# First norm's modulation of a two-block kernel computed in four groups of two operand tiles

## The chip, the cores and the metric

The kernel runs on one core of a Trainium2 chip. The metric is the device time of one execution in microseconds (us), median of the runs; lower is better. Engines: TensorE (PE, with its weight loads as PEld), VectorE (DVE), ScalarE (ACT), GpSimd (POOL) and SyncE (SP), which here issues the transfers.

## What is computed

Only the first norm of the first of two transformer blocks is touched. With D = 1024, S = 512 latent tokens (x) and C = 256 context tokens (ctx):

```python
silu_c = jax.nn.silu(c)
silu_cc = jax.nn.silu(c_ctx)
mod = silu_c @ w_ada[l] + b_ada[l]
mod_c = silu_cc @ w_ada[l] + b_ada[l]
sh1, sc1, gt1, sh2, sc2, gt2 = jnp.split(mod[:, None, :], 6, axis=-1)
h = modulate(rms_norm(x, norm1_g[l]), sh1, sc1)
hc = modulate(rms_norm(xc, norm1_g[l]), csh1, csc1)
... = split_in_proj(h @ w_in[l])
```

`modulate` multiplies by 1 plus the scale and adds the shift. The first norm needs the shift and the scale of layer 0: 2048 columns of `w_ada`, for the two vectors silu(c) and silu(c_ctx). Everything behind the input projection stays as it is.

## The kernel before

**Layout.** Features lie on the 128 partitions, so x is `xL`, eight operand tiles (k = 0 to 7, KD = 8) of 128x512, and ctx is `xC`, eight of 128x256; T = 768 columns together. A full-precision product is made of three products of rounded parts: an operand is split in `high` (rounded) and `low` (the rest), a weight unit in `w_high` and `w_low`. A weight unit is 128x1024 (512 KB), the weights of one output tile for all eight k. It comes through a ring of four (RING = 4) and is split into one of two places (SPLIT = 2): ScalarE copies it to `w_high` (L456), VectorE subtracts to `w_low` (L459).

**First block of code** (L832 to L890). SP issues `small`, `const`, `cond` (the conditioning vectors), x, ctx, then the 16 units of `w_ada` (512 KB each, L646), then four weight units. ScalarE applies silu to `cond`, squares x and ctx (L885), and VectorE adds the squares (L868). TensorE forms the mean (L851), ScalarE an approximate inverse root (L888), VectorE refines it in three steps (L828 to L830) and multiplies every x tile by it into `hL`, `hC` (L874). In between TensorE sums the products of `cond` with `w_ada` (class `Modulation`, L662), 16 matmuls per four units, all into one bank of PSUM. When all 16 units are summed, ScalarE copies the rows out (L676), TensorE turns them into columns (L670: rows to columns by a product with a constant), VectorE adds the bias (L690) and makes the gain from the scale (L696). "Turn" below is this second product.

**The barrier.** Each `nc.Block()` is closed by a barrier of all five engines: nobody, SP included, starts the next block's code until all have reached the end of this one.

**The input projection** (class `Stage`, `input_projection`). Its `normed` part is `Shifted` (L1006): for every k ScalarE makes `high` from `hL`, the gain and the shift. For k in `by_scalar` (2, 4, 6) ScalarE modulates in place (L1025), then rounds (L1028), and VectorE only subtracts (L1043); for the others ScalarE makes `high` in one step (L1031) while VectorE modulates in place (L1040) and subtracts. TensorE (L494, `gemm_tensor`) makes the products of the output tiles 0 and 1 as operands come, tile 1 two operand tiles behind tile 0:

```python
for j in range(n + 2):
    if j < n:
        product(*one, j)
    if j >= 2:
        product(*two, j - 2)
```

One `product` is six matmuls: three pairs of parts, each for 512 and 256 columns. The other 26 tiles follow one by one.

Of the kernel before, what the change touches and what calls it, by code (L numbers as in the profile page):

```python
# [313 lines left out]
def build(nc, dram, where, where1, where2, where3, n_units):  # L314
    with ExitStack() as ctx:
# [156 lines left out]
        def gemm_tensor(pe, g, inner=(), late=None):  # L472
# [31 lines left out]
            if g.paired and g.first == 0:  # L504
# [114 lines left out]
        ada_landed = [count(f"ada_landed{n}") for n in range(5)]  # L619
        ada_used, rows_out, groups_in, mod_out = (count(n) for n in ("ada_used", "rows_out", "groups_in", "mod_out"))  # L620

        class Modulation:

            gpsimd = sync = None
            BANK_AT = 7 * BANK

            def __init__(self, l, block0, blocks, when, places=()):
                self.l, self.block0, self.blocks, self.when, self.places = l, block0, blocks, when, places
                self.units = 2 * blocks
                assert len(when) == self.units and blocks <= 16
                self.last = when[-1]
                self.hooks = self.last + 4

            def load(self, sync, n):
                slot = n % len(self.places)
                if n >= len(self.places):  # L640
                    sync.wait_ge(ada_used.sem, ada_used.at(n - len(self.places) + 1))
                src = dram["ada"][(self.l * 6 * D // ADA_COLS + self.block0) * 2 + n]
                dst = self.places[slot]
                if len(dst.shape) == 3:
                    src = src.rearrange("p (k c) -> p k c", c=ADA_COLS)
                sync.dma_start(dst, src).then_inc(self.landed(n).sem, 16)  # L646

            def landed(self, n):
                return ada_landed[n // 4]

            def wait_landed(self, engine, n):

                engine.wait_ge(self.landed(n).sem, self.landed(n).at(16 * 4))

            def tensor_parts(self, pe, t):
                for n in range(self.units):
                    if self.when[n] == t:
                        self.wait_landed(pe, n)
# [19 lines left out]
            def vector_parts(self, dve, t):  # L678
                if t == self.last + 3:
                    dve.wait_ge(groups_in.sem, groups_in.at(1))  # L680
                    self.finish_columns(dve, ps[:, self.BANK_AT + ADA_COLS:self.BANK_AT + ADA_COLS + 64], 1)

# [2445 lines left out]
```

## Time and profile before

| | |
|---|---|
| runs: median (lowest to highest) | 3451.77 us (3448.72 to 3457.12), n = 3 |
| the profiled execution: its own time | 3454.18 us |
| its span, first to last instruction | 3452.2 us |
| mean granted TensorE clock | 0.989 of full speed |
| TensorE busy | 3307.5 us (96%) |
| VectorE, ScalarE, GpSimd busy | 1771.3 (51%), 1203.1 (35%), 445.2 (13%) us |
| product 0 of the input projection starts | 45.04 us |
| output tile 2 starts | 64.07 us |

Times in the trace count from the first instruction. In a timeline a line is a start, a duration, the engine, the source line, what it writes and reads, how many such instructions were merged, and in brackets the idle time before it with what ended it. In a table of stretches the busy time of each engine is followed by its instruction count, and PEclk is the granted TensorE clock as a share of 2.4 GHz (1.00 is 2.4, 0.50 is 1.2 GHz).

### The profile page before, as it was taken

Reading aid. Unit: us, or ns where it says so; the run is one execution under the profiler, and the core shown is the slowest. Engines: PE = TensorE matmul, PEld = TensorE weight load, DVE = VectorE, ACT = ScalarE, POOL = GpSimd, SP = SyncE. Lnnn points to the kernel's source line nnn. Section 1 sums busy time; section 2 is a strip of 40 time slices with the busy share of each in tenths; the row PEclk is TensorE's granted clock in tenths of the full one; section 3 lists DMA queues with packets and bytes.
Section 4 is the critical chain, followed back from the end, with each engine's and each line's share of the span. In section 5 each row is a group of like instructions: output and inputs, shape, how many; then the busy total and the mean of one; then the engine's idle time right before and its main releaser. Section 6 shows DMA issues by size and latency. Waiting matters only on the chain. (4 is left out here: it accounts for less than half of the span.)

```text
span 3452.2 us, 49601 instructions
## 1 busy us (share of the span) xinstructions
PE 3307.5 (96%) x20432; PEld 2652.1 (77%) x20432; DVE 1771.3 (51%) x2736; ACT 1203.1 (35%) x2054; POOL 445.2 (13%) x477
## 2 busy tenths in 40 slices
PE   6999999999999999999999999999999998899998
PEld 4887778788888787776887867667888777578886
DVE  5874657654132456655323357654443385744433
ACT  3214762321131222753223333353332332532322
POOL 0211111000000021114500133120000022200000
PEclk9999999999999999999999999999999999999999
DMA  6420013354122122012222321012223220022232
GB/s 243 147 99 18 2 50 141 129 188 141 62 68 68 55 86 68 2 50 89 97 92 94 102 84 58 26 43 92 96 94 104 98 86 3 31 98 92 96 100 80
DMA packets 78265, 290.66 MB, mean 84 GB/s; under 512 B 8672, under 2 KB 9056, under 8 KB 77280
## 3 DMA queue, kind: packets, MB, share of 16 engines
q1 hardware_dynamic: 78048, 287.55, 24.5%
q8 instruction: 163, 2.67, 0.3%
q14 instruction: 54, 0.44, 0.0%
HBM read 285.42 MB, written 2.10 MB: 83 GB/s over the span
## 5 line engine op out<-in xcount | busy, mean ns | idle before, releaser
L459 DVE TENSOR_TENSOR w_low<-ring,w_high 128x1024 fp32r<-128x1024 f32 x418 | 526.7, 1260 | 1351.8 <-ACT w_high L456 1351.2
L494 PE MATMUL ps<-arena_r,w_high 128*128 128x512 f32 x3568 | 1142.1, 385 | 11.1 <-PEq L1517 9.2
L456 ACT ACTIVATE w_high<-ring 128x1024 fp32r<-128x1024 f32 x418 | 442.9, 1060 | 1517.9 <-PE ps L494 1508.8
L494 PEld LDWEIGHTS ps<-arena_r,w_high 128*128 128x128 f32 x3568 | 646.1, 188 | 163.7 <-issue 16.7
L494 PE MATMUL ps<-low,w_high 128*128 128x512 f32 (+1 forms) x2448 | 764.7, 361 | 0.0
L494 PE MATMUL ps<-high,w_high 128*128 128x512 f32 x2368 | 737.0, 362 | 15.0 <-DVE low L992 7.0
L494 PE MATMUL ps<-high,w_low 128*128 128x512 f32 x2368 | 730.7, 359 | 0.0
L494 PE MATMUL ps<-arena_r,w_low 128*128 128x512 f32 (+1 forms) x1456 | 545.6, 387 | 0.0
L494 PEld LDWEIGHTS ps<-low,w_high 128*128 128x128 f32 x2448 | 411.7, 189 | 74.8 <-issue 1.1
L494 PEld LDWEIGHTS ps<-high,w_high 128*128 128x128 f32 x2368 | 395.2, 188 | 95.8 <-issue 12.0
L494 PEld LDWEIGHTS ps<-high,w_low 128*128 128x128 f32 x2368 | 395.0, 188 | 70.3
L494 PEld LDWEIGHTS ps<-arena_r,w_low 128*128 128x128 f32 x1456 | 266.6, 189 | 61.3
L555 POOL TENSOR_TENSOR tmp<-tmp 128x512 f32<-128x512 f32 (+1 forms) x42 | 67.3, 1604 | 1527.5 <-ACT tmp L545 1527.5
L1634 ACT ACTIVATE probs<-ps,stat 128x512 f32<-128x512 f32 (+3 forms) x224 | 152.5, 690 | 74.7 <-DVE stat L1592 38.8
L1535 PE MATMUL ps<-arena 64*128 64x256 f32 (+6 forms) x784 | 143.3, 439 | 24.3 <-ACT probs L1634 17.2
L1551 PE MATMUL ps<-const,probs 128*128 128x128 f32 x896 | 125.5, 283 | 13.6 <-ACT probs L1625 6.5
L1551 PEld LDWEIGHTS ps<-const,probs 128*128 128x128 f32 x896 | 100.4, 144 | 49.1 <-DVE probs L1607 36.9
L802 DVE CUSTOM_DVE_ANT_0 arena<-arena 128x1024 f32<-128x1024 f32 x104 | 137.1, 1363 | 0.0
L1535 PEld LDWEIGHTS ps<-arena 64*128 64x128 f32 (+1 forms) x784 | 82.4, 193 | 67.4 <-issue 32.8
L1625 ACT ACTIVATE probs<-ps 128x512 f32<-128x512 f32 (+3 forms) x224 | 121.2, 598 | 22.2 <-PE ps L1551 21.4
L494 PE MATMUL ps<-low,w_low 128*128 128x512 f32 x368 | 127.5, 374 | 0.0
L1564 PE MATMUL ps<-probs,arena 128*64 128x128 f32 x1792 | 123.1, 280 | 2.8 <-ACT hL L1646 2.2
(353 smaller groups left out, 2905.8 us busy)
## 6 DMA issues: line engine op xcount, KB each, us to landing
ring<-in_weights SPq DMA_DIRECT2D x428, 512.0 KB, 3.3
arena<-in_ada_rows SPq DMA_DIRECT2D x80, 512.0 KB, 3.9
arena<-in_ada SPq DMA_DIRECT2D x16, 512.0 KB, 15.5
arena<-in_cond_rows SPq DMA_DIRECT2D x3, 1024.0 KB, 5.8
xL<-in_x SPq DMA_DIRECT2D x1, 2048.0 KB, 10.9
out<-xL SPq DMA_DIRECT2D x4, 512.0 KB, 2.7
low_f<-in_low_rank SPq DMA_DIRECT2D x3, 512.0 KB, 4.2
const<-in_const SPq DMA_DIRECT2D x1, 1104.0 KB, 5.4
```

Of the source, the lines that this page charges most:

```text
L456: act.activation(w_high[:, slot, :], ring[:, place, :], ACT.Copy).then_inc(unit_high.sem, 1)
L459: dve.tensor_tensor(w_low[:, slot, :], ring[:, place, :], w_high[:, slot, :].bitcast(F32), ALU.subtract).then_inc(unit_free.sem, 1)
L494: mm = pe.matmul(bank(4 * (t % 2) + 2 * p + s, width), w, g.split[k][s][x], start=(n == 0 and m == 0), stop=(n == len(part) - 1 and m == 2))
L555: pool.tensor_tensor(tmp[:, 1, 0:total], tmp[:, 1, 0:total], tmp[:, 0, 0:total], ALU.add).then_inc(squares_sum.sem, 1)
L802: ins = dve.tensor_tensor_reduce(out, self.slots[place], self.vectors[s], 1.0, 0.0, ALU.mult, ALU.add, mod[:, to, s:s + 1])
L1535: mm = pe.matmul(ps[:, to:to + w], q, k, start=True, stop=True)
L1551: mm = pe.transpose(ps[:, to:to + P], probs[:, j % 3, e, m * P:m * P + P], con("ident"))
L1564: mm = pe.matmul(ps[e * HD:e * HD + HD, O_AT:O_AT + P], pair["values"][e][m], probs[:, j % 3, e, m * P:m * P + P], start=(m == 0 and not b ...
L1625: act.activation(probs[:, j % 3, e, 0:keys], ps[:, turned_at(j, e):turned_at(j, e) + keys], ACT.Copy).then_inc(turned_out.sem, 1)
L1634: act.activation(probs[:, i % 3, e, 0:keys], ps[:, scores_at(i, e):scores_at(i, e) + keys], ACT.Exp, bias=st[:, 2 + e:3 + e], scale=-1.0, ...
```

## The change

The class `FirstModulation` and the class `Shifted` go; a class `Opening` takes the place of both. The 2048 columns are eight blocks of 256, blocks 0 to 3 the shift and 4 to 7 the scale. Group g (0 to 3) takes block g and block 4 + g, four units of `w_ada`, which give shift and scale of the operand tiles 2g and 2g + 1.

- First block of code: x and ctx are issued first, then `small`, `const`, `cond`, the four units of group 0 and one weight unit. ScalarE squares first and applies silu afterwards. The sums of the modulation and the multiplications by the inverse root are no longer in this block.
- Input projection: SP issues the units of group 1, a weight unit, the units of groups 2 and 3, two weight units. TensorE sums and turns groups 0 and 1, then makes the products; the sums and the turn of group 2 stand ahead of k = 2, those of group 3 ahead of k = 4. Tiles 0 and 1 now go side by side for each k.
- GpSimd multiplies the odd tiles by the inverse root, VectorE the even ones, each ahead of its group's columns. `by_scalar` is (2, 4, 5, 6).

```diff
+            if g.opening:
+                for t in range(2):
+                    begin(t)
+                for k in range(KD):
+                    g.opening.before(pe, k)
+                    for t in range(2):
+                        product(t, 0, k)
+                for t in range(2):
+                    beside(t)
+                done = 2
+            elif g.paired and g.first == 0:
...
+        class Opening:
...
+            by_scalar = (2, 4, 5, 6)
...
+            def open(self, pe, g):
+
+                pe.wait_ge(ada_landed[g].sem, 16 * 4)
+                for m in range(2):
+                    for half in range(2):
+                        unit = self.places[4 * g + 2 * m + half]
+                        for j in range(4):
+                            mm = pe.matmul(ps[32 * j:32 * j + 32, self.region(g):self.region(g) + ADA_COLS],
...
+                mm.then_inc(ada_summed.sem, 1)
+                pe.wait_ge(rows_out.sem, g + 1)
+                for h in range(2):
+                    at = self.region(g) + ADA_COLS + 32 * h
+                    mm = pe.matmul(ps[:, at:at + 32], rows[:, h * P:h * P + P], con("groups"), start=True, stop=True)
+                mm.then_inc(groups_in.sem, 1)
+
+            def tensor(self, pe):
+                for g in range(1 + self.ahead):
+                    self.open(pe, g)
+
+            def before(self, pe, k):
+                g = k // 2 + self.ahead
+                if k % 2 == 0 and k and g < OPEN:
+                    self.open(pe, g)
...
+            def scalar(self, act, gemms, first):
+                for g in range(self.ahead):
+                    self.take_rows(act, g)
+                for g in range(OPEN):
+                    if g + self.ahead < OPEN:
+                        self.take_rows(act, g + self.ahead)
+                    if g == 0:
+                        split_unit(act, None, 0, 0, None, 0)
+                    act.wait_ge(opened.sem, g + 1)
+                    for k in (2 * g, 2 * g + 1):
+                        self.high(act, k, gemms[0].split[k])
+                        if k == 0:
+                            split_unit(act, None, 1, 1, None, 0)
...
+            def vector(self, dve, gemms, first):
+                for g in range(OPEN):
+                    for at, w, x, h in ((0, S, xL, hL), (S, C, xC, hC)):
+                        dve.tensor_tensor(h[:, 2 * g, :], x[:, 2 * g, :], tmp[:, 0, at:at + w], ALU.mult)
+                    self.columns(dve, g)
...
+            def sync(self, sync):
+                for g in range(1, OPEN):
+                    opening.load(sync, g)
+                    load_units(sync, min(g + 1, 2))
+                load_units(sync, RING)
...
+        opening = Opening()
+        opening.ahead = 1
...
             def _(sync):
+                sync.dma_start(xL[:, :, :], dram["x"]).then_inc(tokens_in.sem, 16)
+                sync.dma_start(xC[:, :, :], dram["ctx"]).then_inc(tokens_in.sem, 16)
                 sync.dma_start(small[:, :], dram["small"]).then_inc(params_in.sem, 16)
                 sync.dma_start(const[:, :], dram["const1"]).then_inc(params_in.sem, 16)
                 sync.dma_start(cond[:, :, :], dram["cond"]).then_inc(params_in.sem, 16)
-                sync.dma_start(xL[:, :, :], dram["x"]).then_inc(tokens_in.sem, 16)
-                sync.dma_start(xC[:, :, :], dram["ctx"]).then_inc(tokens_in.sem, 16)
-                first_mod.sync(sync)
-                load_units(sync, RING)
+                opening.load(sync, 0)
+                load_units(sync, 1)
                 sync.wait_ge(params_in.sem, 48)
```

**SP, at the end of the first block.** Before, all of `w_ada` (L646) and the four weight units stand ahead of the barrier:

```order
L646 DMA arena<-in_ada 128x1024 x16
L431 DMA ring<-in_weights 128x1024 x4
L832 UNCONDITIONAL_BRANCH [waits params_in]
L1290 UNCONDITIONAL_BRANCH [waits barrier_Pool_Activation_PE_DVE_SP_release]
L431 DMA ring<-in_weights 128x1024 [waits unit_free]
```

Now (L764 loads `w_ada`, L431 weight units):

```order
L764 DMA arena<-in_ada 128x1024 x4
L431 DMA ring<-in_weights 128x1024
L901 UNCONDITIONAL_BRANCH [waits params_in]
L1300 UNCONDITIONAL_BRANCH [waits barrier_Pool_Activation_PE_DVE_SP_release]
L764 DMA arena<-in_ada 128x1024 x4
L431 DMA ring<-in_weights 128x1024
L764 DMA arena<-in_ada 128x1024 x8
L431 DMA ring<-in_weights 128x1024 x2
```

Groups 1 to 3, 12 of the 16 units, moved behind the barrier.

**ScalarE, from the start of the input projection, now.** L797 copies a group's rows out, L810 makes `high` in one step, L804 and L807 modulate and round:

```order
L1312 UNCONDITIONAL_BRANCH [waits barrier_Pool_Activation_PE_DVE_SP_release]
L797 ACTIVATE rows<-ps 128x256 [waits ada_summed] x2
L456 ACTIVATE w_high<-ring 128x1024 [waits unit_landed0]
L810 ACTIVATE high<-hL,mod,gain 128x512 [waits opened]
L810 ACTIVATE high<-hC,mod,gain 128x256
L456 ACTIVATE w_high<-ring 128x1024 [waits unit_landed1]
L810 ACTIVATE high<-hL,mod,gain 128x512 [waits odd_made]
L810 ACTIVATE high<-hC,mod,gain 128x256
L797 ACTIVATE rows<-ps 128x256 [waits ada_summed]
L804 ACTIVATE hL<-hL,mod,gain 128x512 [waits opened]
L804 ACTIVATE hC<-hC,mod,gain 128x256
L807 ACTIVATE high<-hL 128x512 [waits chain_s]
```

The copies of groups 0 and 1 stand ahead of the first weight unit's split and of k = 0; the copy of group 2 ahead of k = 2, that of group 3 (further on, in the same way) ahead of k = 4.

**TensorE, around the second operand tile's end, now.** L776 sums, L783 turns, L494 is a product; the first row is the last matmul of k = 1 for tile 1:

```order
L494 MATMUL ps<-high,w_low 128x256
L776 MATMUL ps<-arena,cond 32x256 [waits ada_landed2]
L776 MATMUL ps<-arena,cond 32x256 x15
L783 MATMUL ps<-const,rows 128x32 [waits rows_out]
L783 MATMUL ps<-const,rows 128x32
L494 MATMUL ps<-high,w_high 128x512 [waits low_ready]
```

Group 2's sums stand in TensorE's queue behind all four products of k = 0 and 1. Before, no product of the projection had a sum between it and the next.

## Rows read from the trace of the kernel before

**Rows 1.** Page, busy time by engine, and a stretch behind the opening
```profile
PE 3307.5 (96%) x20432; PEld 2652.1 (77%) x20432; DVE 1771.3 (51%) x2736; ACT 1203.1 (35%) x2054; POOL 445.2 (13%) x477
...
50.00:60.00 10.00, 10.00 (x59) 8.86 (x58) 6.67 (x14) 5.15 (x10) 0.00 (x0) 1.00 0.20 80
```
**Rows 2.** TensorE's timeline, sums of the modulation (L662) and the turn (L670)
```profile
20.80 3.64 PE L662 MATMUL ps<-arena,cond 128*32 128x256 f32 x32 [20.80 <-DMA arena<-in_ada]
...
30.94 1.93 PE L662 MATMUL ps<-arena,cond 128*32 128x256 f32 x32 [0.54 <-DMA arena<-in_ada]
...
36.05 3.44 PE L662 MATMUL ps<-arena,cond 128*32 128x256 f32 x32 [3.18 <-DMA arena<-in_ada]
...
40.01 0.63 PE L670 MATMUL ps<-const,rows 128*128 128x32 f32 x4 [0.51 <-ACT rows L676]
```
**Rows 3.** Timeline, from the last sum to the first two products
```profile
39.57 0.38 ACT L676 ACTIVATE rows<-ps 128x256 f32<-128x256 f32 x1 [10.47 <-PE ps L662]
...
41.10 0.24 DVE L696 SCALAR_TENSOR_TENSOR gain<-mod,small 128x8 f32<-128x8 f32 x2
41.62 0.81 ACT L1031 ACTIVATE high<-hL,mod,gain 128x512 fp32r<-128x512 f32 x1 [0.72 <-PEq L832]
...
45.04 0.98 PE L494 MATMUL ps<-high,w_high 128*128 128x512 f32 x2 [4.40 <-DVE low L1043]
...
47.09 1.00 PE L494 MATMUL ps<-high,w_high 128*128 128x512 f32 x2
```
**Rows 4.** Stretches of two us around the sums and first products; columns end PEclk, DMA share, GB/s
```profile
36.00:38.00 2.00, 1.95 (x20) 0.99 (x24) 2.00 (x5) 0.00 (x0) 0.00 (x0) 0.50 1.03 412
...
46.00:48.00 2.00, 2.00 (x8) 1.50 (x7) 1.99 (x3) 1.97 (x5) 0.00 (x0) 0.50 1.00 414
...
50.00:52.00 2.00, 2.00 (x13) 1.79 (x12) 2.00 (x5) 2.00 (x5) 0.00 (x0) 1.00 0.93 381
```
**Rows 5.** Transfers: KB each, median us from issue to landing
```profile
cond<-in_cond SPq DMA_DIRECT2D x1, 248.0 KB, 6.5
...
ring<-in_weights SPq DMA_DIRECT2D x428, 512.0 KB, 3.3
```
**Rows 6.** Timeline of the first block: ScalarE's squares, VectorE's sums, the root's last step
```profile
15.56 0.63 ACT L885 ACTIVATE hL<-xL 128x512 f32<-128x512 f32 x1 [6.78 <-DMA xC<-in_ctx]
...
17.36 0.69 DVE L868 TENSOR_TENSOR tmp<-hL 128x512 f32<-128x512 f32 x1 [9.02 <-ACT hC L885]
...
24.76 0.42 DVE L868 TENSOR_TENSOR tmp<-tmp,hC 128x256 f32<-128x256 f32 x1
...
31.12 0.96 DVE L830 SCALAR_TENSOR_TENSOR tmp<-tmp 128x768 f32<-128x768 f32 x1
```
**Rows 7.** SP's waits, 0 to 50 us: for whom, total, times, longest
```profile
SPq L832 <- PEq L832: 15.7, 1, 15.7
```
**Rows 8.** Groups by form: VectorE's modulation to 66 us, GpSimd's nearest rows in the span
```profile
L1040 DVE TENSOR_SCALAR hL<-hL,gain,mod 128x512 f32<-128x512 f32 x5 | 2.7, 545 | 0.5 <-ACT high L1031 0.4
...
L1040 DVE TENSOR_SCALAR hC<-hC,gain,mod 128x256 f32<-128x256 f32 x5 | 2.0, 410 | 0.0
...
L555 POOL TENSOR_TENSOR tmp<-tmp 128x512 f32<-128x512 f32 (+1 forms) x42 | 67.3, 1604 | 1527.5 <-ACT tmp L545 1527.5
```
**Rows 9.** Timeline, making of the operand tile k = 4 by ScalarE and VectorE
```profile
48.34 0.80 ACT L1025 ACTIVATE hL<-hL,mod,gain 128x512 f32<-128x512 f32 x1
...
50.20 0.40 ACT L1028 ACTIVATE high<-hC 128x256 fp32r<-128x256 f32 x1
...
51.47 0.42 DVE L1043 TENSOR_TENSOR low<-hC,high 128x256 fp32r<-128x256 f32 x1
```
**Rows 10.** Timeline, third weight unit and output tile 2
```profile
61.09 1.06 ACT L456 ACTIVATE w_high<-ring 128x1024 fp32r<-128x1024 f32 x1 [5.91 <-PE ps L494]
62.18 1.23 DVE L459 TENSOR_TENSOR w_low<-ring,w_high 128x1024 fp32r<-128x1024 f32 x1 [5.04 <-ACT w_high L456]
...
64.07 0.61 PE L494 MATMUL ps<-high,w_high 128*128 128x512 f32 x2
```

More of the change, by code:

```diff
@@ L503, in gemm_tensor @@
             done = 0
-            if g.paired and g.first == 0:
+            if g.opening:
[9 more added lines that the diff above has]
+            elif g.paired and g.first == 0:
                 one, two = ((0, 0), (0, 1)) if len(g.parts) == 2 else ((0, 0), (1, 0))
@@ L706, in build @@
-        class FirstModulation(Modulation):
-            def sync(self, sync):
-                for n in range(self.units):
-                    self.load(sync, n)
+        OPEN = 4
+        ada_landed = [count(f"ada_landed{n}") for n in range(OPEN)]
+        ada_summed, rows_out, groups_in, bias_in, opened, odd_made = (
+            count(n) for n in ("ada_summed", "rows_out", "groups_in", "bias_in", "opened", "odd_made"))
         cond_in, cond_made, row_used = (count(n) for n in ("cond_in", "cond_made", "row_used"))
@@ L871, in _ @@
                 inverse_root(dve, tmp[:, 0, :], ps[:, 5 * BANK:5 * BANK + T], EPS, tmp[:, 1, :])
-                for k in range(KD):
-                    for at, w, x, h in ((0, S, xL, hL), (S, C, xC, hC)):
-                        dve.tensor_tensor(h[:, k, :], x[:, k, :], tmp[:, 0, at:at + w], ALU.mult)
-                for t in range(first_mod.hooks):
-                    first_mod.vector_parts(dve, t)
             @block.scalar
             def _(act):
-                act.wait_ge(params_in.sem, 48)
-                act.activation(cond[:, :, :], cond[:, :, :], ACT.Silu).then_inc(left_s.sem, 1)
                 act.wait_ge(tokens_in.sem, 32)
@@ L886, in _ @@
                     ins.then_inc(squares_in.sem, 1)
+                act.wait_ge(params_in.sem, 48)
+                act.activation(cond[:, :, :], cond[:, :, :], ACT.Silu).then_inc(left_s.sem, 1)
                 act.wait_ge(pe_ready.sem, 1)
@@ L1169, in __init__ @@
                     g.made, g.own = made, 0 if made else len(g.split)
+                    g.opening = None
                 first = 0
@@ L1349, in input_projection @@
                 gemms.append(g)
-            return Stage(gemms, ToZ(), normed, inner=[Heads(l), *also])
+            stage = Stage(gemms, ToZ(), normed, beside, inner=[Heads(l), *also])
+            if normed is opening:
+                gemms[0].opening = opening
+            return stage
         values_turned, values_out, sq_out, mean_in, mean_read, root_out, normed_out = (count(n) for n in (
@@ L1996, in build @@
                      [(19, 0, 2 * KD, 3 * KD, 2 * KD, 2, 1)], True, 18)
-        project([input_projection(0, Shifted(lambda k, s: gain[:, 0, k, s:s + 1], lambda k, s: mod[:, k, s:s + 1]), [CondRows(cond0, 0), rows0])])
+        project([input_projection(0, opening, [CondRows(cond0, 0), rows0], FirstLoads())])
         for l in range(DEPTH):
```

198 lines of the change are left out of this document (76 added, 122 removed).

## The prediction

> **What bounds the kernel.** I read the page first, then the table of stretches, the waits and the timeline up to 66 us. TensorE is busy for 96% of the span, and from the first products on it has no idle time: a stretch of ten us behind the opening has 10.00 us of it [rows 1]. So the kernel is an opening, in which TensorE waits, and then a queue of products. What the opening costs is the time at which output tile 2 starts. All behind it hangs on TensorE's tiles (weights, evictions, later sums), so a shift of that start goes one to one into the end.
>
> The opening before is bound by transfers. The sums of 16 matmuls wait for `w_ada` three times; the last begin at 36.05 and end at 39.49 [rows 2]. Rows and turn follow, the gain is ready at 41.34, ScalarE's first `high` starts at 41.62, and the first product stands at 45.04 [rows 3].
>
> **What moves, in order of time.** All times are those of the trace of before, from the first instruction.
>
> *Tokens first.* `small`, `const` and `cond` are 126 + 1104 + 248 KB, 1.51 MB; at 0.41 MB per us (last column of [rows 4]) x and ctx land 3.7 us sooner, at 11.8 instead of 15.5. But VectorE waits for `cond` ahead of its sums, and that was there at 8.15 (1.65 + 6.5 [rows 5]) and now lands last of the five, at 15.5. Its sums start at 15.7 instead of 17.36 [rows 6]: a gain of 1.7 us, not 3.7. They end at 23.5, the root's last step 6.9 us later as before (25.18 to 32.08 [rows 6]), at 30.4. Silu and its table load on ScalarE lie in these sums and cost nothing; without that cover they would cost about 2 us.
>
> *The barrier.* SP now issues group 0 and one weight unit and waits. That it does wait is seen before: 15.7 us at the block's end, at no cost, since all transfers were issued [rows 7]. Now groups 1 to 3 are issued only when the root is done, at 30.4 + 0.3 (41.34 to 41.62 is such a passage [rows 3]) = 30.7. The queue has run dry meanwhile. A 512 KB transfer takes 3.3 us to land [rows 5], each further one 1.28 us at 410 GB/s: group 1 lands at 30.7 + 3.3 + 3 x 1.28 = 37.9.
>
> *First product.* Group 0 is summed meanwhile. Group 1's sums stand ahead of the products on TensorE, and its copy ahead of the first split and `high` on ScalarE. Its sums take 1.93 us at 2.4 and 3.44 at 1.2 GHz [rows 2, 4]; TensorE has idled before, so I take 3.44: 41.4. The copy takes 0.46 (39.49 to 39.95 [rows 2, 3]), the split 1.06, and from ScalarE's first `high` to the product are 3.42 [rows 3]: 46.4 instead of 45.04, **1.4 us later**.
>
> *GpSimd's multiplications.* Their cost is bounded by 0 and by 8 x 1.6 = 13 us [rows 8]: from 30.7 they end at 44 at the latest, the one for k = 1 at 34, when ScalarE wants it at 45. Nothing; without this cover, up to 3 us.
>
> *In the groups.* A product takes 2.05 us at 1.2 GHz (45.04 to 47.09 [rows 3]) and half, 1.03, at 2.4. k = 0 and 1 are four products, the first two at the low clock: 46.4 to 52.6. Behind them TensorE sums group 2, 1.93 us, to 54.5. Only then can ScalarE copy the rows (0.46), and behind the copy in its queue stands the making of k = 2, although its gain may be long there: 48.34 to 50.60 in the row, 2.3 us, then VectorE's subtraction and the hand-over, 1.2 [rows 9]. TensorE has nothing in this time but the turn (0.6): a gap of 3.95 us, new. k = 2 and 3 take 4.1, with operands in time: for k = 3 ScalarE needs 1.3 and VectorE 0.96 + 1.1 [rows 6, 8], which is a product pair's 2.06. The same comes again ahead of k = 4. Ahead of k = 6 no sums are left, but VectorE multiplies and makes the columns only behind the `low` of k = 5 (1.0 + 0.7 [rows 2, 3, 6]), and then the 2.3 and 1.2 run again: 5.2 us less the 2.06 of products, a gap of 3.15. Last, the third weight unit's split waits for tile 0. It takes 2.3 us (61.09 to 63.41 [rows 10]; tile 2 then started at 64.07); before, three products of tile 1 covered it, now one does: 1.3 us.
>
> **Sum.** Later start 1.4; sums inside the products 2 x 1.93 = 3.9; gaps 2 x 3.95 + 3.15 = 11.05; third unit 1.3; together 17.6. To this comes the clock. Before, idle times of 3.18 and 4.40 us were both followed by 0.50 in PEclk [rows 2, 3, 4], and the products from 45.04 ran at 1.2 GHz for their first four us, a loss of 2 us. The gaps here are as long, two of them broken by the turn. Bounds: none falls, 0; all three fall, 6. I take two of three at 1.6, 3.2, since the gaps are nearest to the one of 3.18, after which the 3.44 of the sums cost 1.5 over 1.93. The sum is **+20.8 us**.
>
> On the clock the Trainium skill ("TensorE: Matmul & The Clock Gate", section "HAM oscillation — how this bites in real kernels") speaks against this change: a loop that computes briefly and then waits falls back to the low clock at each wait. The trace agrees as far as it goes (both its idle times). By the rule all three gaps fall, and the sum would be 23.6 instead of 20.8.
>
> The profiled execution has 3454.18 us, so 3475.0; it stands 2.4 above the median of the runs, to which the change is compared: **3472**.
>
> **Rivals.** A measurement of this kernel can tell 0.3%, 10.4 us, from no change.
>
> *A, the forecast:* chance 0.65. Its own bounds: no fall of the clock (-3.2), group 1 summed at 2.4 GHz (-1.5), transfers 1 us quicker or slower, three falls (+2.8), 2 us from GpSimd and the first copies: 3464 to 3480.
>
> *B, the low clock stays all through the opening.* The 14 products that I put at 1.03 take 2.05, +14, and the two sums inside +3, less the 3.2: 3486. For it: a rise took four us of unbroken work at 45 us, and no stretch here is longer. Against it: the products from 45.04 on were at 1.00 in the stretch from 50 us [rows 4], and those from 46.4 on follow each other here without a pause just as long. 0.10.
>
> *C, group 1 isn't waited for*, because SP passes the barrier or its transfers start at once (then the change's barrier does not do what the order says). Then the first product would come when group 0's sums (34.2) are copied, turned and used: 34.2 + 2.1 + 3.4 = 39.7, 6.7 sooner; 3465. Against it is SP's wait [rows 7]. Still slower, since gaps and sums stay. 0.12.
>
> *D, no change: the gaps close.* The place is ScalarE's queue ahead of k = 2, 4 and 6. If the rows come out and the operand tiles are made while TensorE still has products or sums, the 11 us of gaps and the 3.2 of clock go: 3458, within 0.3%; with C as well 3451. It decides at 2 us: the copy, `high` and `low` would have to end within the sums they wait for. For it: ScalarE is only half busy [rows 1]. Against: the copy waits for the sums' end, and 0.46 + 2.3 + 1.2 follow one upon the other. 0.09.
>
> *E, transfers bind.* Groups 2 and 3 land at 44 and 49, 8 and 13 us ahead of their sums, w2 and w3 at 50 and 52. They would have to run at under half of 410 GB/s: 3480 or more. 0.04.
>
> **Numbers.** Range 3461 to 3483: A with its bounds, C, and the upper edge of E; outside are B and D. Faster by over 0.3% (under 3441) no case gives: 0.01. Within 0.3%: D and a little of C, 0.10. Slower: 0.89.
>
> **What would show it.** Right: SP's first `w_ada` transfer behind the barrier at 31 us; first product at 46 to 47; ahead of k = 2 and k = 4 an idle time of TensorE of 3 to 4 us in two pieces around the turn, ended by the copy and by `low`; one of about 3 ahead of k = 6; tile 2 starting at 82 to 86; from there equal spacing of tiles. Wrong: a first product under 42 (C); gaps under 1 us (D); PEclk 0.50 over all of 46 to 80 (B); sums of groups 2 and 3 that wait for transfers (E); or tile 2 at its old place relative to the end, with the difference made elsewhere.

## The result, and the profile after

| | before | after |
|---|---|---|
| runs: median (lowest to highest) | 3449.55 us (3447.78 to 3457.12), n = 5 | 3471.82 us (3465.57 to 3472.75), n = 5 |
| profiled execution: own time, span | 3454.18, 3452.2 us | 3472.75, 3471.0 us |
| mean granted TensorE clock | 0.989 | 0.990 |
| product 0 of the input projection | 45.04 us | 45.88 us |
| output tile 2 starts | 64.07 us | 83.47 us |
| ScalarE's table load inside the projection (L1424, now L1437) | 126.64 us | 147.58 us |

The ratio is 1.0055, with a 95% interval of 1.004 to 1.007: slower by 14 to 24 us. The last row of the table is used as a mark below: it is one instruction of the projection, the same in all kernels here, and what stands ahead of it is the opening and the first tiles.

The page of the changed kernel has TensorE's busy time almost unchanged (3307.5 before [rows 1]); the first slices carry the difference:

```profile
span 3471.0 us, 49648 instructions
...
PE 3310.5 (95%) x20444; PEld 2659.2 (77%) x20444; DVE 1767.9 (51%) x2744; ACT 1206.5 (35%) x2060; POOL 453.8 (13%) x485
```

TensorE's timeline of the changed kernel, 18 to 95 us, answers to [rows 2, 3, 10]; L776 are sums, L783 turns, L494 products:

```profile
22.82 2.90 PE L918 MATMUL ps<-tmp,const 128*128 128x512 f32 x4 [22.82 <-DVE tmp L934]
30.17 3.64 PE L776 MATMUL ps<-arena,cond 128*32 128x256 f32 x32 [4.45 <-PEq L901]
34.30 1.06 PE L783 MATMUL ps<-const,rows 128*128 128x32 f32 x4 [0.49 <-ACT rows L797]
37.54 3.64 PE L776 MATMUL ps<-arena,cond 128*32 128x256 f32 x32 [2.18 <-DMA arena<-in_ada]
41.69 1.06 PE L783 MATMUL ps<-const,rows 128*128 128x32 f32 x4 [0.50 <-ACT rows L797]
45.88 0.98 PE L494 MATMUL ps<-high,w_high 128*128 128x512 f32 x2 [3.13 <-DVE low L860]
...
51.78 1.93 PE L776 MATMUL ps<-arena,cond 128*32 128x256 f32 x32
54.22 0.63 PE L783 MATMUL ps<-const,rows 128*128 128x32 f32 x4 [0.50 <-ACT rows L797]
57.43 1.01 PE L494 MATMUL ps<-high,w_high 128*128 128x512 f32 x2 [2.58 <-DVE low L860]
...
64.31 1.93 PE L776 MATMUL ps<-arena,cond 128*32 128x256 f32 x32
66.75 0.63 PE L783 MATMUL ps<-const,rows 128*128 128x32 f32 x4 [0.50 <-ACT rows L797]
69.97 1.01 PE L494 MATMUL ps<-high,w_high 128*128 128x512 f32 x2 [2.58 <-DVE low L860]
...
76.98 0.61 PE L494 MATMUL ps<-high,w_high 128*128 128x512 f32 x2 [1.11 <-DVE low L860]
...
83.47 1.01 PE L494 MATMUL ps<-high,w_high 128*128 128x512 f32 x2 [2.04 <-DVE arena L1344]
```

Read it from the brackets. The sums of group 1 end a wait for a transfer, at 37.54. Ahead of k = 2 (57.43) and k = 4 (69.97) the same pattern stands twice: sums, 0.50 us of waiting for ScalarE's copy, the turn, 2.58 us of waiting for a `low` tile. Ahead of k = 6 it is 1.11 us, and tile 2 waits 2.04 us for VectorE's eviction of tile 0 (L1344). None of these waits was there before, between 45.04 and 64.07.

ScalarE's timeline of the changed kernel shows the order that makes the gap: the copy comes first, then the tile whose gain has long been there.

```profile
45.33 0.59 ACT L810 ACTIVATE high<-hC,mod,gain 128x256 fp32r<-128x256 f32 x1
53.78 0.38 ACT L797 ACTIVATE rows<-ps 128x256 f32<-128x256 f32 x1 [7.87 <-PE ps L776]
54.06 0.80 ACT L804 ACTIVATE hL<-hL,mod,gain 128x512 f32<-128x512 f32 x1
...
55.92 0.40 ACT L807 ACTIVATE high<-hC 128x256 fp32r<-128x256 f32 x1
```

It was idle for 7.87 us, the last 3.6 of them with the gain of group 1 ready: VectorE had it at 50.19.

```profile
49.96 0.23 DVE L841 SCALAR_TENSOR_TENSOR gain<-mod,small 128x2 f32<-128x2 f32 x2
```

The table of stretches shows the clock behind three of the gaps:

```profile
58.00:60.00 2.00, 2.00 (x8) 1.68 (x7) 1.97 (x5) 0.00 (x0) 0.00 (x0) 0.50 0.21 84
70.00:72.00 2.00, 2.00 (x6) 1.71 (x7) 0.95 (x3) 0.99 (x3) 0.00 (x0) 0.50 0.00 0
84.00:86.00 2.00, 2.00 (x8) 1.65 (x7) 0.00 (x0) 2.00 (x3) 0.00 (x0) 0.50 0.69 242
```

The column misses one stretch at the low clock. The row of the first products reads 1.00:

```profile
46.00:48.00 2.00, 2.00 (x7) 1.72 (x8) 1.97 (x4) 0.00 (x0) 0.00 (x0) 1.00 1.03 412
```

But from 46.66 to 49.22 one pair of matmuls follows the other every 0.64 us, as it does where the column has 0.50, and from 49.61 on every 0.35 us, as it does where the column has 1.00. So these products, too, began at 1.2 GHz.

**The sum of it up to the mark** (147.58 - 126.64 = 20.9 us). I split the time from the first product to the mark in stretches of 1 us and added up TensorE's idle time, and its busy time times the share of the clock that was missing (busy at PEclk 0.50 counts half as loss): idle 9.3 us against 0.0 before, clock 5.9 against 2.2, the rest 86.4 against 79.4. With the first product 0.8 us later that is 0.8 + 9.3 + 3.8 + 7.0 = 20.9. Of the 7.0, the two sums and turns inside the products are 2 x (1.93 + 0.63) = 5.1, and 1.5 are clock as well, from the stretch that the column misses: the first six pairs of matmuls took 3.73 us (45.88 to 49.61), six pairs at 2.4 GHz took 2.19 (76.98 to 79.17). So the clock's loss up to the mark is 7.5 us, 5.3 more than before; 0.4 us are left over.

Behind the mark the two profiled executions differ in something that the change doesn't touch. Between the marks at 289.47 and 482.93 us before, and 310.40 and 500.25 after, the distance falls from 20.9 to 17.3 us. The stretch there is the start of the attention, before:

```profile
295.00:305.00 10.00, 8.85 (x45) 7.04 (x43) 5.05 (x11) 5.20 (x13) 0.00 (x0) 0.50 0.00 0
```

and after:

```profile
316.00:326.00 10.00, 7.97 (x58) 6.34 (x57) 6.23 (x14) 6.47 (x15) 0.29 (x1) 0.83 0.00 0
```

The kernel before stayed at 1.2 GHz for these ten us, the changed one for a part of them. In the nine experiments below the ten us at the same place, of the same code, have 0.53 to 0.89. From the mark to the end the eleven profiled executions take 3318.9 to 3325.6 us, and the one of the kernel before is the longest. So the experiments are read by tile 2 and the mark, where effects of 2 us show, and only then by the time.

### The profile page after: what moved, and what is told of

Its sections match the earlier page's. It is cut to its first block and busy times, and to the rows that moved or that the text cites. A ratio compares the mean times of both kernels' runs of the same rounds, so it can differ in the third digit from the quotient of the medians.

```text
span 3471.0 us, 49648 instructions
## 1 busy us (share of the span) xinstructions
PE 3310.5 (95%) x20444; PEld 2659.2 (77%) x20444; DVE 1767.9 (51%) x2744; ACT 1206.5 (35%) x2060; POOL 453.8 (13%) x485
## 5 line engine op out<-in xcount | busy, mean ns | idle before, releaser
L494 PE MATMUL ps<-arena_r,w_high 128*128 128x512 f32 x3568 | 1143.3, 386 | 11.1 <-PEq L1530 9.1
L494 PEld LDWEIGHTS ps<-arena_r,w_high 128*128 128x128 f32 x3568 | 647.2, 188 | 162.5 <-issue 16.7
L494 PE MATMUL ps<-low,w_high 128*128 128x512 f32 (+1 forms) x2448 | 767.4, 362 | 0.0
L494 PE MATMUL ps<-high,w_high 128*128 128x512 f32 x2368 | 739.7, 363 | 23.5 <-DVE low L860 9.4
L494 PE MATMUL ps<-high,w_low 128*128 128x512 f32 x2368 | 732.5, 360 | 0.0
L494 PE MATMUL ps<-arena_r,w_low 128*128 128x512 f32 (+1 forms) x1456 | 546.4, 388 | 0.0
L494 PEld LDWEIGHTS ps<-high,w_high 128*128 128x128 f32 x2368 | 397.1, 189 | 103.0 <-issue 10.9
L494 PEld LDWEIGHTS ps<-low,w_high 128*128 128x128 f32 x2448 | 413.8, 190 | 74.5 <-issue 1.1
L494 PEld LDWEIGHTS ps<-high,w_low 128*128 128x128 f32 x2368 | 396.8, 189 | 70.2
L494 PEld LDWEIGHTS ps<-arena_r,w_low 128*128 128x128 f32 x1456 | 267.1, 189 | 61.1
L494 PE MATMUL ps<-low,w_low 128*128 128x512 f32 x368 | 127.6, 375 | 0.0
```

Of the source, the lines that this page charges most:

```text
L494: mm = pe.matmul(bank(4 * (t % 2) + 2 * p + s, width), w, g.split[k][s][x], start=(n == 0 and m == 0), stop=(n == len(part) - 1 and m == 2))
```

## The experiments

All times of the mark, tile 2 and first product are from the profiled executions. The ratios compare medians. For the changed kernel the kernel before had 3449.55 us (n = 5); in the experiments it was measured again beside each of them and had 3452.1 to 3452.6 (n = 12 to 21). Against these the changed kernel's median is 19 to 20 us over, not 22.

| kernel | first product | tile 2 | mark | span | ratio to before, interval |
|---|---|---|---|---|---|
| before | 45.04 | 64.07 | 126.64 | 3452.2 | |
| changed | 45.88 | 83.47 | 147.58 | 3471.0 | 1.0055, 1.004 to 1.007 |
| transfers ahead | 43.60 | 80.98 | 143.55 | 3463.8 | 1.0036, 1.0021 to 1.005 |
| and all groups first | 49.66 | 77.83 | 140.40 | 3460.6 | 1.0031, 1.002 to 1.0043 |
| tile 1 lags | 46.81 | 85.05 | 147.62 | 3469.3 | 1.004, 1.0026 to 1.0055 |
| gaps filled | 46.41 | 83.92 | 146.49 | 3466.9 | 1.0054, 1.0038 to 1.0071 |
| before, tokens first | 46.05 | 65.80 | 128.37 | 3450.0 | 1.0001, 0.9992 to 1.0011 |
| spread | 39.06 | 66.82 | 129.39 | 3454.0 | 1.0004, 0.9995 to 1.0013 |
| spread, no GpSimd | 35.77 | 60.41 | 123.00 | 3441.9 | 0.9984, 0.9975 to 0.9993 |
| changed, sums don't wait | 45.45 | 82.63 | 145.22 | 3468.6 | 1.0039, 1.0024 to 1.0054 |
| spread, both | 35.07 | 58.17 | 120.75 | 3443.5 | 0.9978, 0.9968 to 0.9987 |

### 1. The transfers ahead of the barrier

```diff
                 opening.load(sync, 0)
                 load_units(sync, 1)
+                for g in range(1, OPEN):
+                    opening.load(sync, g)
+                    load_units(sync, min(g + 1, 2))
+                load_units(sync, RING)
                 sync.wait_ge(params_in.sem, 48)
```

> The changed kernel with the transfers of groups 1 to 3 and of the weight units issued in the first block, ahead of the barrier. Theory (late start from group 1's transfers is one of three costs, gaps and sums inside the products the others): group 1 is there when group 0 is turned, its sums start at about 35.4 us instead of 37.5, run partly at 2.4 GHz, first product at 42.5 to 44 instead of 45.9, gaps of TensorE ahead of k = 2 and 4 as before (about 3.7 us), tile 2 at 80 to 82 instead of 83.5: 2 to 3 us less than the changed kernel, about 17 us over the kernel before. Rival (the barrier makes most of the loss): first product near 40, gaps gone or short because the later groups are early, at most 8 us over the kernel before.

TensorE's timeline of this kernel, groups 1 and 2:

```profile
35.35 3.55 PE L776 MATMUL ps<-arena,cond 128*32 128x256 f32 x32
39.41 0.63 PE L783 MATMUL ps<-const,rows 128*128 128x32 f32 x4 [0.51 <-ACT rows L797]
43.60 0.98 PE L494 MATMUL ps<-high,w_high 128*128 128x512 f32 x2 [3.56 <-DVE low L860]
...
56.03 1.01 PE L494 MATMUL ps<-high,w_high 128*128 128x512 f32 x2 [2.58 <-DVE low L860]
```

Group 1's sums wait for no transfer any more (35.35 instead of 37.54), the first product comes 2.3 us sooner, tile 2 2.5 us, the mark 4.0 us. The wait of 2.58 us ahead of k = 2 is the same to the last digit. So the late transfers cost 2.3 to 2.5 us. The other 1.5 us at the mark are the clock, which this time didn't fall behind the wait ahead of tile 2: from tile 2 to the mark it is 62.57 us instead of 64.11. The rival that gives the barrier most of the loss falls: 16.9 us are left at the mark, and the median is 12.4 over that of the kernel before, where the rival had at most 8.

### 2. All four groups ahead of the products

```diff
             def region(self, g):
-                return (7, 3)[g % 2] * BANK
+                return (7, 3, 6, 2)[g] * BANK
...
-        opening.ahead = 1
+        opening.ahead = 3
```

on top of experiment 1.

> As the kernel with the early transfers, and in addition the sums and turns of all four groups stand ahead of the first product (four regions of PSUM instead of two). Theory (the chain sums, copy, operand, low part between the products is the main cost): first product later, at 48 to 50 us, but no sums and no gap over 0.5 us ahead of k = 2, 4, 6; tile 2 at 70 to 72; 6 to 9 us over the kernel before, so some 12 us less than the changed kernel although its products start later. Rival (the later start and transfers are the cost, the gaps come from slow operand making on ScalarE and VectorE): gaps of 3 us stay ahead of each even k, 20 us or more over the kernel before.

TensorE's timeline of this kernel:

```profile
49.66 0.98 PE L494 MATMUL ps<-high,w_high 128*128 128x512 f32 x2 [3.56 <-DVE low L860]
57.39 0.61 PE L494 MATMUL ps<-high,w_high 128*128 128x512 f32 x2 [2.02 <-DVE low L860]
64.34 0.62 PE L494 MATMUL ps<-high,w_high 128*128 128x512 f32 x2 [2.49 <-DVE low L860]
71.34 0.62 PE L494 MATMUL ps<-high,w_high 128*128 128x512 f32 x2 [2.50 <-DVE low L860]
```

A first product 6.1 us later than in experiment 1, and yet tile 2 3.2 us sooner. From the first product to tile 2 it is 28.2 us instead of 37.4: sums, copies and turns between the products cost 9.2 us, the falls of the clock behind their waits included. But I expected no gap, and 2.0 to 2.5 us are left ahead of every even k. ScalarE's timeline of this kernel names who is late:

```profile
54.00 0.82 ACT L804 ACTIVATE hL<-hL,mod,gain 128x512 f32<-128x512 f32 x1 [4.31 <-DVE gain L841]
...
60.95 0.81 ACT L804 ACTIVATE hL<-hL,mod,gain 128x512 f32<-128x512 f32 x1 [3.47 <-DVE gain L841]
```

It waits for the gain, though all columns were turned by 46.1 us: VectorE multiplies tile k and makes the columns only behind the `low` of the tile ahead. So there are two chains: sums, copy, operand (TensorE to ScalarE), and low, multiplication, columns, operand (VectorE to ScalarE). Taking the first away brings the time from k = 1's end to k = 2's start from 5.65 us in the changed kernel (51.78 to 57.43) down to 2.0. The median is 10.9 us over the kernel before, where I expected 6 to 9.

### 3. Tile 1 two operand tiles behind

```diff
-                for k in range(KD):
+                for k in range(KD + 2):
                     g.opening.before(pe, k)
-                    for t in range(2):
-                        product(t, 0, k)
+                    if k < KD:
+                        product(0, 0, k)
+                    if k >= 2:
+                        product(1, 0, k - 2)
```

> The changed kernel with tile 1 two operand tiles behind tile 0, as in the kernel before, nothing else. Theory (the third unit's split and tile 0's eviction are covered by one product of tile 1 where three covered them): the idle 2.0 us ahead of tile 2 go, and the fall of the clock behind it; the gaps ahead of k = 2 and 4 shrink a little or stay, since fewer products stand behind the sums; tile 2 at 80 to 81.5 at 2.4 GHz, 3 to 4 us less than the changed kernel over the opening. Rival (the idle time is the silu or the transfer of the unit): tile 2 still starts 2 us behind the last product of tile 1.

A miss: tile 2 starts at 85.05, where I expected 80 to 81.5. The idle 2.04 us ahead of tile 2 did go, with the low clock behind them, as expected. But the mark stands where it did (147.62; 0.9 us of it is group 1, which landed later in this execution: its sums began at 38.48 instead of 37.54). With the lag, only two products stand ahead of group 2's sums, the others behind the gap, and the gap stays at 2.58 us:

```profile
49.70 1.01 PE L494 MATMUL ps<-high,w_high 128*128 128x512 f32 x2 [0.63 <-DVE low L862]
...
51.91 3.18 PE L778 MATMUL ps<-arena,cond 128*32 128x256 f32 x32
55.61 0.63 PE L785 MATMUL ps<-const,rows 128*128 128x32 f32 x4 [0.51 <-ACT rows L799]
58.82 1.01 PE L494 MATMUL ps<-high,w_high 128*128 128x512 f32 x2 [2.58 <-DVE low L862]
```

The sums took 3.18 instead of 1.93 us, since the clock had not risen by then. Up to the mark TensorE is idle for 7.8 us instead of 9.3, and the clock's loss is 8.1 instead of 7.5. So 0.6 of the 1.5 us that the lag saved went to the clock and the other 0.9 to the late group 1.

### 4. The gaps filled with matmuls

```diff
                 if k % 2 == 0 and k and g < OPEN:
                     self.open(pe, g)
+                    for m in range(3):
+                        pe.matmul(bank(6), con("mean_all"), const[:, 0:BANK], start=True, stop=True)
```

> The changed kernel with three matmuls of 512 columns into an unused bank behind the turns of groups 2 and 3, so that TensorE works through the two long gaps (2.6 us of 2.4 GHz work each). Theory (the clock falls in the gaps and costs 2 to 3 us in each): PEclk stays 1.00 from 50 to 75 us, the products of k = 2 to 5 take 1.03 us each, tile 2 at 79 to 80 instead of 83.5, 3 to 5 us less. Rival (the clock's fall is hidden since operands are the bound at either clock): tile 2 where it is, 83.5, or later by what the added matmuls delay.

TensorE's timeline of this kernel; L795 are the added matmuls:

```profile
55.72 0.63 PE L783 MATMUL ps<-const,rows 128*128 128x32 f32 x4 [0.50 <-ACT rows L799]
56.18 2.82 PE L795 MATMUL ps<-const 128*128 128x512 f32 x6
58.93 0.61 PE L494 MATMUL ps<-high,w_high 128*128 128x512 f32 x2
...
63.31 1.93 PE L776 MATMUL ps<-arena,cond 128*32 128x256 f32 x32
...
68.96 0.61 PE L494 MATMUL ps<-high,w_high 128*128 128x512 f32 x2
...
75.97 1.01 PE L494 MATMUL ps<-high,w_high 128*128 128x512 f32 x2 [2.49 <-DVE low L862]
```

The clock held 1.00 from 54 to 74 us, as meant. From group 2's sums to group 3's it is 10.0 us (53.28 to 63.31) instead of 12.5 (51.78 to 64.31): the first fall's price, 2.5 us. From group 3's sums to k = 6 it is 12.7 us with and without the fill (63.31 to 75.97, 64.31 to 76.98): the products are quicker, and the gap ahead of k = 6 is longer, 2.49 instead of 1.11. There the rival holds, operands are the bound. Tile 2 is 0.45 us later, the mark 1.1 sooner; this execution's first product was 0.5 later and its first four products ran 1 us longer at the low clock. But the clock now fell behind the longer gap:

```profile
76.00:78.00 2.00, 2.00 (x6) 1.71 (x7) 1.88 (x4) 0.05 (x1) 0.00 (x0) 0.50 0.00 0
```

From k = 6 to tile 2 it is 7.95 us instead of 6.49, and with that 1.5 us more; from tile 2 to the mark, where the clock stayed up, it is 62.57 instead of 64.11, 1.5 us less. So a fall costs 1.5 to 2.5 us where TensorE is the bound behind it, and nothing where a later wait shrinks by as much; filling the two gaps moved one fall to k = 6.

### 5. The kernel before with the tokens first

The kernel before, x and ctx ahead of `small`, `const` and `cond`, squares ahead of silu:

```diff
+                sync.dma_start(xL[:, :, :], dram["x"]).then_inc(tokens_in.sem, 16)
+                sync.dma_start(xC[:, :, :], dram["ctx"]).then_inc(tokens_in.sem, 16)
                 sync.dma_start(small[:, :], dram["small"]).then_inc(params_in.sem, 16)
...
-                sync.dma_start(xL[:, :, :], dram["x"]).then_inc(tokens_in.sem, 16)
-                sync.dma_start(xC[:, :, :], dram["ctx"]).then_inc(tokens_in.sem, 16)
```

> The kernel before with one part of the change alone: x and ctx issued first, squares ahead of silu. Theory (the opening of the kernel before is bound by the last group's landing, which no order of the same bytes moves): the root is done 2 us sooner, the last sums still start at 36.0 and the first product at 45.0; no change, within 3 us. Rival (the tokens are the bound): first product and end 2 us or more sooner.

The root's last step starts at 28.70 instead of 31.12, and nothing comes of it: the last sums start at 36.44 after a wait of 3.57 us for `w_ada`, the first product at 46.05. 1.0001, interval 0.9992 to 1.0011. The part of the change that is a gain by itself is worth nothing while the last unit's landing is the bound.

### 6. The groups with their order spread

All transfers ahead of the barrier, group 0 summed and turned in the first block, sums and turns apart, copies behind a tile that is made, GpSimd multiplying tiles 1 to 7, tile 1 two behind:

```diff
             def tensor(self, pe):
-                for g in range(1 + self.ahead):
-                    self.open(pe, g)
+                self.sums(pe, 1)
+                self.sums(pe, 2)
+                self.turn(pe, 1)

             def before(self, pe, k):
-                g = k // 2 + self.ahead
-                if k % 2 == 0 and k and g < OPEN:
-                    self.open(pe, g)
+                if k == 1:
+                    self.turn(pe, 2)
+                if k == 2:
+                    self.sums(pe, 3)
+                if k == 4:
+                    self.turn(pe, 3)
...
+                for k in range(KD):
+                    if k % 2 == 0:
+                        act.wait_ge(opened.sem, k // 2 + 1)
+                    self.high(act, k, gemms[0].split[k])
+                    if k == 0:
+                        self.take_rows(act, 1)
+                        split_unit(act, None, 1, 1, None, 0)
+                    if k == 1:
+                        self.take_rows(act, 2)
+                    if k == 3:
+                        self.take_rows(act, 3)
```

> The changed kernel with its groups kept and the order rewritten: all transfers ahead of the barrier, group 0 summed and turned in the first block, sums and turn of a group at separate places (sums of 1 and 2 and turn of 1 ahead of k = 0, turn of 2 ahead of k = 1, sums of 3 ahead of k = 2, turn of 3 ahead of k = 4), ScalarE's copies behind a tile that is already made, GpSimd multiplying tiles 1 to 7, tile 1 two behind. Theory (the groups can gain once nothing on ScalarE waits for sums that stand behind products): first product at 35 to 37 us, no gap over 1 us except at the start, tile 2 at 57 to 60 instead of 64.07, 4 to 7 us under the kernel before (0.1 to 0.2%). Rival 1 (ScalarE and VectorE can't make operands in the products' time with GpSimd's part beside them): gaps of 1 to 2 us per tile, tile 2 at 64 or later, no gain. Rival 2 (sums through the transfers bind): sums of group 2 or 3 wait, tile 2 at 62.

17 us sooner at tile 2 than the changed kernel, and no different from the kernel before (1.0004, 0.9995 to 1.0013). The first rival shows, in a form that I hadn't thought of. VectorE's timeline of this kernel, the `low` tile of k = 0 beside GpSimd and that of k = 2 after it:

```profile
34.14 1.50 DVE L862 TENSOR_SCALAR hL<-hL,gain,mod 128x512 f32<-128x512 f32 x1
...
36.42 1.63 DVE L865 TENSOR_TENSOR low<-hL,high 128x512 fp32r<-128x512 f32 x1
...
38.84 2.30 DVE L459 TENSOR_TENSOR w_low<-ring,w_high 128x1024 fp32r<-128x1024 f32 x1
...
48.81 0.69 DVE L865 TENSOR_TENSOR low<-hL,high 128x512 fp32r<-128x512 f32 x1 [2.34 <-ACT high L817]
```

The same instructions take 0.54, 0.69 and 1.22 us when GpSimd stands still. GpSimd worked from 31.18 to 48.3, and TensorE waited 5.15 us for the `low` tile of k = 1 at 45.85 (the text recorded for experiment 7 calls it the third operand tile; it is the second).

### 7. The same without GpSimd

```diff
+            def turned(self, dve, k):
+                for at, w, x, h in ((0, S, xL, hL), (S, C, xC, hC)):
+                    ins = dve.tensor_tensor(h[:, k, :], x[:, k, :], tmp[:, 0, at:at + w], ALU.mult)
+                ins.then_inc(odd_made.sem, 1)
...
             def gpsimd(self, pool):
-                for k in range(1, KD):
-                    for at, w, x, h in ((0, S, xL, hL), (S, C, xC, hC)):
-                        ins = pool.tensor_tensor(h[:, k, :], x[:, k, :], tmp[:, 0, at:at + w], ALU.mult)
-                    ins.then_inc(odd_made.sem, 1)
+                pass
```

> The spread kernel with all multiplications by the inverse root on VectorE, none on GpSimd. Theory (GpSimd's eight-odd multiplications slowed VectorE's instructions beside them, 0.69 to 1.63 us for a 128x512 subtraction, and that made the 5 us gap ahead of its third operand tile): VectorE's subtractions stay at 0.69 us from 31 to 48 us, first product at 36 instead of 39, last low part at 56 to 57 instead of 62.4, tile 2 at 59 to 61 instead of 66.8; 3 to 5 us under the kernel before. Rival (VectorE was the bound by its own work, and seven more multiplications of 0.94 us make it worse): tile 2 at 67 or later, no gain.

VectorE's timeline of this kernel, the instructions of the fence above:

```profile
33.70 0.54 DVE L868 TENSOR_SCALAR hL<-hL,gain,mod 128x512 f32<-128x512 f32 x1
...
34.60 0.69 DVE L871 TENSOR_TENSOR low<-hL,high 128x512 fp32r<-128x512 f32 x1
...
35.54 1.22 DVE L459 TENSOR_TENSOR w_low<-ring,w_high 128x1024 fp32r<-128x1024 f32 x1
```

With seven more multiplications on VectorE its last `low` tile is done at 55.98 instead of 62.37, tile 2 starts at 60.41, and the kernel is faster than the one before: 0.9984, interval 0.9975 to 0.9993. At the mark it is 3.6 us ahead. Beside the multiplications one thing more differs: VectorE makes the columns of group 2 one tile sooner. That GpSimd slowed VectorE is shown by the single instructions; how much of the 6.4 us at tile 2 is the columns is not shown.

### 8. The changed kernel, sums not waiting for the parameters

```diff
-                dve.wait_ge(params_in.sem, 48)
-
-                dve.tensor_tensor(col("attn0", 0, KD), col("final1", 0, KD), col("attn0", 0, KD), ALU.mult)
...
+                dve.wait_ge(params_in.sem, 48)
+
+                dve.tensor_tensor(col("attn0", 0, KD), col("final1", 0, KD), col("attn0", 0, KD), ALU.mult)
                 dve.wait_ge(act_ready.sem, 1)
```

> The changed kernel with VectorE's wait for the parameters, and the small product behind it, moved behind the sums of squares. Theory (of the 3.7 us by which the tokens land sooner, this wait takes two): sums from 12.8 us, at their end by 20.7, mean at 20.8, barrier, first w_ada transfer behind it and first product 2 us sooner (28.0 and 43.8), tile 2 at 81 to 82; 2 us less than the changed kernel. Rival (silu and the two table loads on ScalarE or the constants for the mean are next and give only part): 1 us or less.

Between the two expectations. The sums started only 1.1 us sooner, at 13.73 instead of 14.86, since the tokens landed 0.8 us later in this execution (squares from 11.94, not 11.09), and the root gained those 1.1 us. Group 1 was issued 1.1 us sooner (29.00) and landed no sooner (sums at 37.46), so the first product gained 0.4. The mark is 2.4 us sooner, of which 1.5 are the clock, which didn't fall ahead of tile 2 (62.59 us from there to the mark, not 64.11). The step isn't settled by this kernel; in the next one, where the tokens landed in time, the mean comes 2.0 us sooner.

### 9. Both

Experiment 7 with the edit of experiment 8.

> The kernel without GpSimd's multiplications with the parameters' wait moved as well. Theory: root and first product another 2 us sooner (34), last operand tiles bound by VectorE's own queue from there, tile 2 at 57.5 to 59; 5 to 7 us under the kernel before, 0.15 to 0.2%. Rival (group 2's and 3's landing at 31 and 36 us is next): the sums of group 2 wait on transfers and tile 2 stands where it does without this edit.

The mean starts at 20.87 instead of 22.90. The first product gains only 0.7 us of that: its `low` tile is there at 33.59, but group 2's sums, which wait 0.36 us for their transfer (the rival, small), and the turn of group 1 stand ahead of it to 35.1. Tile 2 starts at 58.17, 2.2 us sooner than in experiment 7; 1.5 of these are the clock, which fell there behind a wait of 2.17 us ahead of k = 1 and here doesn't. The mark is at 120.75, 5.9 us ahead of the kernel before. In the table of stretches of this kernel the clock stays up from 35 to 55 us, and TensorE is busy for 17.6 of these 20 us:

```profile
35.00:45.00 10.00, 8.19 (x69) 6.17 (x69) 9.69 (x32) 6.43 (x13) 0.00 (x0) 1.00 1.02 410
45.00:55.00 10.00, 9.43 (x55) 7.86 (x54) 7.03 (x20) 5.49 (x10) 0.00 (x0) 1.00 0.21 84
```

Median 3443.72 us against 3452.1, ratio 0.9978, interval 0.9968 to 0.9987. It has the lowest median of all kernels here, though its interval and that of experiment 7 overlap. VectorE is what is full now (9.69 of 10 us up to 45). Of the 8.4 us, 5.9 stand at the mark; the rest is behind it and not explained by the edits.

## Why the prediction was right

The forecast was 3472 us, 20.8 us over the profiled execution; measured were 3471.82 and, between the profiled executions, 18.6 (3472.75 - 3454.18). (3475.0 less the 2.4 is 3472.6, which the prediction wrote as 3472.) The late start, the sums inside the products and the gaps are where it put them; the clock, the gap ahead of k = 6 and the third unit were mis-sized and made up for each other. Step by step:

- **Tokens first.** VectorE's sums were held by the parameters as said; they ended at 22.67 instead of 23.5, as the parameters landed 0.7 us sooner than I had worked out.
- **The barrier.** SP's first `w_ada` transfer behind it came at 30.13 (said: 31), group 1's sums at 37.54 (37.9). Experiment 1 confirms the step and prices it at 2.3 us at the first product.
- **First product.** 45.88 instead of 46.4.
- **The sums inside the products.** 2 x 1.93 us, as said.
- **GpSimd: nothing.** Right for this kernel: its last multiplication ended at 38.57, the first was wanted at 44.62. GpSimd's and VectorE's first instructions slowed each other (L848, 256 columns, 1.50 instead of 0.42 us), in a time in which VectorE had nothing to do. That GpSimd's work has a price on VectorE was no part of my step, and experiment 6 ran into it.
- **The gaps ahead of k = 2 and 4.** Said 3.95, turn included; measured 3.72 and 3.73 from the sums' end to the product (53.71 to 57.43, 66.24 to 69.97).
- **The gap ahead of k = 6, said 3.15, was 1.11.** The chain was right, the products beside it weren't: I let them run at 2.4 GHz, and in this profile they ran partly at 1.2 (5.90 us for the four of k = 4 and 5, where four take 4.16 at 2.4 GHz), which fills the gap. Experiment 4 shows the two as one term: with the clock held up the gap is 2.49 and the time from group 3's sums to k = 6 the same. I had counted gap and clock there twice.
- **The third unit, said 1.3, was 2.04.** The step left out the eviction of tile 0, 0.68 us on VectorE between `w_low` and tile 2 (L1344 in TensorE's bracket). And the clock fell behind this wait as well, which no step had.
- **The clock, said 3.2 for two of three gaps, was 5.3.** It fell behind the first two and behind the wait ahead of tile 2. The four products of k = 2 and 3 took 6.88 us instead of 4.16, those of k = 4 and 5 5.90, and the stretch from tile 2 to the mark 64.11 instead of 62.57: 2.7, 1.7 and 1.5 us; the first four products lost 0.5 less than before (5.9 us, not 6.4). I had put a fall at 1.6, from the sums of one group; experiment 4 prices the first at 2.5. The Trainium skill's rule ("TensorE: Matmul & The Clock Gate", section "HAM oscillation — how this bites in real kernels"), by which each wait in such a loop brings the low clock, was the better guide for the two long gaps, behind which the clock fell both times. The trace doesn't bear it out for the gap ahead of k = 6: behind its 1.11 us idle the stretch from 78 to 80 us has 1.00, and in experiment 2, where gaps of 2.0 to 2.5 us stand ahead of each even k, the products behind them ran at 1.00.

So the clock was 2.1 us and the third unit 0.7 too small, the gap ahead of k = 6 2.0 and the other gaps and the start 1.0 too large. They came to 20.8 together, where tile 2 shows 19.4 and the mark 20.9. That the median fell on the forecast to 0.2 us is luck: of the 20.9 at the mark the profiled executions keep 18.6 at the end, and the five runs of the changed kernel spread over 7 us. The forecast's range and its mechanism were right, the single number was better than its terms.

Of the rivals, B (low clock throughout) and E (transfers bind) are not in the profile. C priced the first product at 39.7 if group 1 weren't waited for; experiment 1 has 43.60: C forgot that group 1's sums still stand ahead of the first product. D, the gaps close, was dismissed for the changed kernel rightly. Experiments 7 and 9 make most of it true by moving ScalarE's copies, TensorE's turns and VectorE's columns: 2.7 and 2.4 us of idle time are left between the first product and the mark.

## What to carry to other kernels

When work is cut into groups so that it can overlap, put on paper for every engine what stands behind the group's waits in its queue: here sums, copies and turns in the products' way cost 9.2 us (experiment 2), the late transfers 2.3 (experiment 1). Taking the pieces apart (sums, copy, turn, columns), placing each one product behind its input and issuing the transfers ahead of the barrier took away the loss of 0.5% (experiment 6); with the multiplications off GpSimd it became a gain of 0.2% (experiments 7 and 9), all with the same arithmetic. And measure an idle engine's help on the engine beside it before counting it as free.

## What the runs showed of the hardware

- GpSimd and VectorE slowed each other when they worked at the same time: a VectorE subtraction of 128x512 took 1.63 instead of 0.69 us, a 128x1024 one 2.30 instead of 1.22, a one-input modulation 1.50 instead of 0.54, and GpSimd's multiplication up to 2.26 instead of 1.27 us (experiments 6 and 7; the 1.27 is the changed kernel's, beside an idle VectorE). The Trainium skill ("SBUF — State Buffer", section "Who interferes with whom") says that the two share a pair of ports under an exclusive lock, which a VectorE instruction with two inputs in SBUF or in a two-port mode needs, and that the later one is blocked while the other's instruction holds it. These numbers agree with it: what is added, 0.94 to 1.08 us, is never longer than one instruction of the other. Whether the one-input modulation ran in such a mode no view here shows.
- The clock fell after the wait of 2.04 us ahead of tile 2 in the changed kernel; after the same wait of 2.04 us in experiments 1, 4 and 8 it stayed up. After a wait of 2.49 us ahead of k = 6 it fell in experiment 4, after those of 2.49 and 2.50 us in experiment 2 it stayed up. The length of a wait alone doesn't decide it in these runs.
- PEclk can read 1.00 in the first stretches of a trace while the matmuls run at 1.2 GHz: in the changed kernel from 30 us to 49 us, with a group's sums in 3.64 us where they take 1.93 at 2.4 GHz, and products whose pairs come every 0.64 us where they come every 0.35. Check the column against the durations before adding it up.
- The time from the issue of group 1's four 512 KB transfers to its first sum was 7.4 us in the changed kernel (30.13 to 37.54) and 8.3, 7.7 and 8.5 us in experiments 3, 4 and 8, with the same order of transfers. What makes the difference of about 1 us is not shown.
